# A delta rule's VectorE order, and the last steps of a small inversion on GpSimd, in a float32 transformer kernel

## What is computed

```python
def gated_delta_rule(q, k, v, g, beta):
    ...
    kb = kc * bc[..., None]
    A = jnp.where(strict, jnp.einsum('nbhid,nbhjd->nbhij', kb, kc) * decay, 0.0)
    rhs = jnp.concatenate([vc * bc[..., None], kb * jnp.exp(G)[..., None]], axis=-1)
    sol = lax.linalg.triangular_solve(A + jnp.eye(CHUNK, dtype=A.dtype), rhs, ...)
    ...
    def step(S, xs):
        u_c, w_c, q_c, qk_c, k_c, gl = xs
        v_new = u_c - jnp.einsum('bhck,bhkv->bhcv', w_c, S)
        o = jnp.einsum('bhck,bhkv->bhcv', q_c, S) + jnp.einsum('bhij,bhjv->bhiv', qk_c, v_new)
        S = gl * S + jnp.einsum('bhck,bhcv->bhkv', k_c, v_new)
        return S, o
```

```python
def head_group_norm(t, g):
    mu = jnp.mean(t, axis=-1, keepdims=True)
    var = jnp.mean(jnp.square(t - mu), axis=-1, keepdims=True)
    return (t - mu) * lax.rsqrt(var + NORM_EPS) * g.astype(jnp.float32)
```

## Time and profile before

| | |
|---|---|
| median of 3 runs | 1374.26 us (1373.92 to 1382.46) |
| the profiled execution, its own time | 1378.08 us |
| span of its trace | 1376.3 us |
| busy: PE, PEld, DVE, ACT, POOL | 1286.7, 1097.0, 905.7, 695.6, 103.7 us |
| chain that ended last, by engine | PE 80%, DVE 10%, ACT 5%, POOL 2%, issue 2% |

### The profile page before, as it was taken

How to read it: one execution, slowest core, us unless ns; L and a number is a source line. 1 busy time by engine, 2 the same in 40 slices (tenths; PEclk the granted TensorE clock), 3 DMA queues, 4 the chain that set the end, 5 groups by cost and what they waited for, 6 DMA issues and landing times.

```text
span 1376.3 us, 18712 instructions
## 1 busy us (share of the span) xinstructions
PE 1286.7 (93%) x7504; PEld 1097.0 (80%) x7504; DVE 905.7 (66%) x1395; ACT 695.6 (51%) x1132; POOL 103.7 (8%) x165
## 2 busy tenths in 40 slices
PE   6999999898999999989999999999988879899997
PEld 4899987877888887976888877777877876688886
DVE  4454544346888867676888876755775666666665
ACT  4444444345766655565666755343471114544553
POOL 1000000001000001001000001021370300000000
PEclk9999999999999999999999999999998999999999
DMA  9644333545645557427555547112523105455551
GB/s 352 256 148 165 133 122 129 198 163 215 229 183 184 184 183 269 175 99 292 190 185 184 184 184 265 70 62 105 193 98 92 31 1 182 185 190 185 184 204 65
DMA packets 31780, 231.10 MB, mean 168 GB/s; under 512 B 10912, under 2 KB 14624, under 8 KB 18768
## 3 DMA queue, kind: packets, MB, share of 16 engines
q1 hardware_dynamic: 25616, 218.66, 43.5%
q10 hardware_dynamic: 5072, 7.61, 1.6%
q0 software_dynamic: 1008, 3.67, 0.7%
HBM read 226.22 MB, written 3.71 MB: 167 GB/s over the span
## 4 chain that ended last, share of the span: by engine, by line
PE 80%; DVE 10%; ACT 5%; POOL 2%; issue 2%; DMA 0%; DVEq 0%; POOLq 0%; ACTq 0%
PE ps L425 19%; PE ps L597 15%; PE ps L476 10%; PE ps L197 10%; PE ps L429 10%; PE ps L467 5%; PE ps L564 4%; PE ps L536 3%; PE ps L508 3%; DVE parts L333 2%; ACT parts L329 2%; POOL row L1035 1%; POOL arena L1032 1%; DVE arena L279 1%; ACT arena L231 1%
## 5 line engine op out<-in xcount | busy, mean ns | idle before, releaser
L333 DVE TENSOR_TENSOR parts<-ring,parts 128x1024 fp32r<-128x1024 f32 x354 | 432.9, 1226 | 284.0 <-ACT parts L329 219.2
L329 ACT ACTIVATE parts<-ring 128x1024 fp32r<-128x1024 f32 x354 | 373.2, 1057 | 296.0 <-PE ps L429 107.7
L425 PE MATMUL ps<-hall,parts 128*128 128x512 f32 x1120 | 399.3, 401 | 6.6 <-DVE hall L282 5.1
L429 PE MATMUL ps<-hall,parts 128*128 128x256 f32 x1120 | 315.3, 282 | 0.0
L597 PE MATMUL ps<-parts 128*128 128x512 f32 x1128 | 264.0, 393 | 12.8 <-DVE parts L364 10.6
L597 PEld LDWEIGHTS ps<-parts 128*128 128x128 f32 x1128 | 211.1, 189 | 63.1 <-DVE parts L364 16.4
L425 PEld LDWEIGHTS ps<-hall,parts 128*128 128x128 f32 x1120 | 211.3, 189 | 62.6 <-DVE hall L282 3.5
L429 PEld LDWEIGHTS ps<-hall,parts 128*128 128x128 f32 x1120 | 212.6, 190 | 0.0
L197 PE MATMUL ps<-arena 128*128 128x128 f32 (+3 forms) x1014 | 140.9, 299 | 29.0 <-DVE arena L2037 10.7
L197 PEld LDWEIGHTS ps<-arena 128*128 128x128 f32 (+2 forms) x1014 | 128.0, 194 | 40.0 <-DVE arena L2037 11.3
L476 PE MATMUL ps<-hall,parts 128*128 128x256 f32 x1152 | 140.4, 284 | 0.7 <-ACT arena L1113 0.7
(11 more groups left out here) (229 smaller groups left out, 1066.3 us busy)
## 6 DMA issues: line engine op xcount, KB each, us to landing
ring<-in_W SPq DMA_DIRECT2D x100, 2048.0 KB, 8.1
arena<-distance_tables SPq DMA_DIRECT2D x8, 384.0 KB, 7.9
gains<-in_gains POOLq DMA_DIRECT2D x5, 512.0 KB, 6.5
ring<-in_W SPq DMA_DIRECT2D x4, 512.0 KB, 8.9
arena<-in_gate_w ACTq DMA_DIRECT2D x1, 2048.0 KB, 10.1
matrices<-arena ACTq DMA_DIRECT2D x8, 256.0 KB, 2.8
x<-in_x SPq DMA_DIRECT2D x1, 1024.0 KB, 5.8
gates<-in_ada_gate_b POOLq DMA_DIRECT2D x2, 512.0 KB, 5.3
```

Source lines behind the costliest of these rows:

```text
L329: return nc.scalar.activation(unit_weights(n, 0, weights), weights, ACT.Copy)
L333: return nc.vector.tensor_tensor(unit_weights(n, 1, weights), weights, unit_weights(n, 0, weights), ALU.subtract)
L425: last = nc.tensor.matmul(ps[:, b, :].rearrange("p (a b) -> p a b", a=2), w[:, 0, :], hparts[:, :, k, :], start=k == 0, stop=False)
L429: last = nc.tensor.matmul(ps[:, b, 0:S], w[:, 1, :], hparts[:, 0, k, :], start=False, stop=k == KT - 1)
```

## The change

There are two parts. In the loop the diff reorders VectorE and splits one semaphore:

- the residual R comes behind the level-0 masks and `Rv`, ahead of the level-0 subtractions; so does the retention's centre in step 0
- the level-0 subtraction of `XT` now waits for X·Y alone (PE signals it apart), and each of the two subtractions adds one to `X_out`; PE starts the last level's Y when `XT`'s subtraction is done and does not wait for `X`'s; the last Z (and the query-key products of steps 2 and 3) wait for `X`'s
- nothing stands between the last level's copies and its subtractions. `ET`'s mask follows them; the norm's first half follows them in step 1; the variance and the gates stand at the end of step 0; the norm's other half at the end of step 1; weight splitting late in step 3
- VectorE waits for the step before's `vnew` behind the masks, not ahead of them

In the small inversion GpSimd does all steps: k = 1 to 14, the two `inverse_length`, k = 15 to 30, and the diagonal. ScalarE makes the reversed copy, ahead of the gate's tanh of the retention (`gate_tanh(w_rg, rgt)`), and adds the second `inverses`; SP's first store waits for the first `inverses`, the second store for the second.

```diff
         def first_turned(step, d):
             return 6 * step + 2 * d + 1
         def first_whole(step, d):
             return 6 * step + 2 * d + 2
         def last_turned(step, d):
             return 6 * step + 5 + d
...
-            substitute(1, 11)
+            substitute(1, 15)
             for i in range(TT2, TT2 + TT):
                 inverse_length(i)
-            substitute(11, POOL_STEPS)
+            substitute(15, BLK - 1)
+            nc.gpsimd.memset(WHOLE[:, 0:BLK * BLK:BLK + 1], -1.0).then_inc(S_("inverses"), 1)
...
+            act.wait_ge(S_("inverses"), 1)
+            nc_a.activation(turned_out[SECOND_DIR].rearrange("p i j -> p (i j)"), WHOLE[SECOND_DIR, ::-1], ACT.Copy).then_inc(S_("inverses"), 1)
             act.wait_ge(S_("tok_vector"), TT2 + 2 * TT)
             gate_tanh(w_rg, rgt)
...
-            dve.wait_ge(S_("inverse_step"), 2 * POOL_STEPS - 1)
-            for k in range(POOL_STEPS, BLK - 1):
...
-            link(v.memset(WHOLE[:, 0:BLK * BLK:BLK + 1], -1.0))
-            v.tensor_copy(turned_out[SECOND_DIR].rearrange("p i j -> p (i j)"), WHOLE[SECOND_DIR, ::-1]).then_inc(S_("inverses"), 1)
...
+                for d in DIRS:
+                    xt, xx = half(XT[d], 0, d == 0), half(X[d], 0, d == 1)
+                    dve.wait_ge(S_("Z"), first_turned(step, d))
+                    v.tensor_tensor(xt, xt, half_bank(4 * d + 1, 0, d == 0), ALU.subtract).then_inc(S_("X_out"), 1)
+                    dve.wait_ge(S_("Z"), first_whole(step, d))
+                    v.tensor_tensor(xx, xx, half_bank(4 * d + 2, 0, d == 1), ALU.subtract).then_inc(S_("X_out"), 1)
...
                         if l:
-                            pe.wait_ge(S_("X_out"), level(step, l - 1, d))
+                            pe.wait_ge(S_("X_out"), first_turned(step, d))
...
                         if l == LAST:
+                            pe.wait_ge(S_("X_out"), first_whole(step, d))
...
-                            heads(4 * d + 1, X[d], Ys[l][d])
+                            heads(4 * d + 1, X[d], Ys[l][d]).then_inc(S_("Z"), 1)
                             heads(4 * d + 2, Ys[l][d], X[d]).then_inc(S_("Z"), 1)
...
                 for d in DIRS:
-                    pe.wait_ge(S_("X_out"), level(step, LEVELS - 1, d))
+                    pe.wait_ge(S_("X_out"), last_turned(step, d))
```

98 lines of the change are left out of this document (48 added, 50 removed).

## The result

| | before | after |
|---|---|---|
| median, us | 1380.01 (1373.77 to 1385.78, 7 runs) | 1366.66 (1363.44 to 1369.78, 7 runs) |
| ratio, 95% interval | | 0.9914 (0.9893 to 0.9936) |
| the profiled execution, us | 1378.08 | 1369.78 |

The changed kernel is faster by 0.86%, 11.8 us of 1374, where 18.5 were predicted. The median of the kernel before over these seven runs is 5.75 us above that of the three shown ahead of the prediction, so the ratio is the fairer measure: 1374.26 x 0.9914 = 1362.4 us. The forecast, 1355.8, was too low either way, and the median of 1366.66 lies above the stated range, which ended at 1362.5.

The account below looks back on a forecast made before the run. TensorE idles for VectorE (10.7 us at last-level subtractions, 5.3 at the first `weighed`), then runs at half speed. Inversion 5.9 + loop 10.5 + clock 1.9 and 0.2 = 18.5 us off 1374.26: 1355.8 us, range 1351.3 to 1362.5.

Parts of the forecast that it names:

- Part 1: Small inversion: GpSimd does all steps, so step 0's transposes start earlier; gain 5.9 us, from 3.1 to 7.7.
- the normalizing of the queries: VectorE's reader of the later inverse lengths: delay costs nothing behind a projection, 3 us if that cover fails.
- the clock of step 0: TensorE's half speed in step 0: +1.8 or -1.5 us at about even chances, together +0.2.
- The loop's 1.5 us: Delta loop, step 0: the centre ends earlier, so vnew can start at 1059.3 instead of 1060.78.
- The lower end of my range: Whole kernel: inversion gain at 7.7 us and both clock terms good, 23 us gained, 1351.3 us.
- step 2's miss: Delta loop, step 2: 3.3 us from the wait, less about 0.5 for the later state, 2.8 us gained.
- R ends behind the arrival of Z: Delta loop: sign of being wrong; R was to end at 1073.3 in step 1, hidden behind Z.
- the masks of step 2 wait for VectorE's norm: Delta loop, step 2: sign of being wrong, if a mask waits for the norm.
- Step 1: Delta loop: 4.5 us from the idle time and an earlier Y, plus 1.9 us of clock.
- Step 3: Delta loop: gain of 1.48 + 0.45 = 1.9 us up to vnew.
- The hand-over: Behind step 3's vnew: the weight splitting stands ahead of the output, costing 0.2 us.
- the clock falls in every step all the same: Rival, 12%: small matrices and waits at each level keep half speed; gain 13.4 us, 1360.9 us.

Follow-up runs that it names:

- after_again: The changed kernel itself, measured once more beside its two parts: 1364.2 us, ratio 0.9904.
- whole_wait: The changed kernel, but TensorE's last-level Y waits for both level-0 subtractions of its direction again: 1366.49 us, ratio 0.9917.
- residual_back: The changed kernel with the residual R moved back behind the last copies in steps 1 to 3: 1365.48 us, ratio 0.9909.
- loop_only: The changed kernel with the small inversion of before, so only the delta loop's order is changed: 1366.34 us, ratio 0.9914.
- keys_wait: The changed kernel with GpSimd's decayed keys waiting for both expansions in steps 0 and 2: 1360.49 us, ratio 0.9878.
- centre_early: The changed kernel with the sums and scaling of the retention's centre ahead of step 0's level-0 masks: 1360.87 us, ratio 0.9892.
- combined: The changed kernel with early centre sums, GpSimd's keys waiting in steps 0 to 2, and eight unread multiplications ahead of step 0: 1358.17 us, ratio 0.9863.
- fill_before: The changed kernel with eight unread 128x128 multiplications ahead of the first transposes of step 0: 1362.3 us, ratio 0.9904.
- qk_late: The changed kernel with the query-key products of steps 2 and 3 behind vnew on TensorE's queue: 1365.54 us, ratio 0.9916.
- combined_fill3: As combined, with ten more unread multiplications ahead of the transposes of step 3: 1355.69 us, ratio 0.9832.
- combined_no_fill: As combined, without its unread multiplications: 1362.26 us, ratio 0.9856.

## Why the prediction was wrong

**Part 1** was right as a mechanism and in size. GpSimd's k = 23 to 30 took 1038.13 - 1029.87 = 8.3 us against 8.5, VectorE's first `weighed` starts as scores 0 are done (S + 2.1 us), the four issues take 1.94 us instead of 3.36, and the transposes wait for `expand` and it for the DMAs: 6.1 us between S and T0 against 5.9. That it is so near is partly luck: `expand` starts 0.8 us earlier after S than my sum has it (15.2 against 16.1), since the issues are shorter, and its first half takes longer than the 0.65 us that I had, since the keys are beside it. In `after_again` the gain was 4.8 us. The projection cost 0.7 us (M to S) where I had nothing, and not for the reason that I had weighed: the normalizing of the queries kept its cover, but GpSimd's added steps stand beside VectorE's instructions that read SBUF twice. VectorE's instruction ahead of that projection, before (L1764) and after (L1776), and TensorE behind it:

```profile
997.96 0.69 DVE L1764 TENSOR_TENSOR arena<-arena 128x512 f32<-128x512 f32 x1
```

```profile
1004.33 1.17 DVE L1776 TENSOR_TENSOR arena<-arena 128x512 f32<-128x512 f32 x1
```

```profile
1005.55 11.18 PE L564 MATMUL ps<-parts,hall 128*128 128x512 f32 x48 [1.56 <-DVE arena L1776]
```

TensorE waited 0.67 us there before; the rows do not show more of the cause than that the two engines worked side by side. The other kernels with this inversion have the loss too (46.4 to 46.7 us from M to S, and 48 in `whole_wait` and `residual_back`, against 45.7 and 45.8 for the two without). In the two with 48, TensorE waits 3.14 us at that place and then takes 12.8 us for the same 48 records, not 11.2: clock, where in after none was lost.

**The step that failed is the clock of step 0**: "either can go either way: +1.8 and -1.5 at about even chances, together +0.2". The loop's 1.5 us less the 1.8 us that the step grew makes the term -3.3 us in this trace, and -2.5 in `after_again`. The 3.5 us between +0.2 and -3.3 are half of the 6.9 by which the traces miss the sum. Two things were wrong in it. I took the 1.8 us that half speed cost before as something to be won and 1.5, for which I had no row, as the most that could be lost, though the idle time ahead of the transposes stands ahead of the whole step and not of 32 records; from 14.4 us at full clock the step went up to 19.2, 4.9 us. And I counted the idle time within the step as something that might keep the old loss, not as one that could add to it: the centre ended at 1059.0 and level 0 waited 1.20 us for it, behind which the second stretch fell, 9.26 us against 6.40. `loop_only` has no idle time ahead of the transposes, `keys_wait` less of it (1.29 us), `centre_early` none within the step, and their steps take 14.4, 14.4 and 14.8 us.

More generally, I let gains go through without asking who arrives first where they meet: the inversion's path was still late last, by 2 to 3 us, so all that `weighed` saved beyond it became idle time of TensorE, ahead of a step of small matrices.

The lower end of my range was also added up wrong: 18.5 with 1.8 more of part 1 and 1.6 more of the clock makes 21.9 us, not 23.

**Collisions** in the loop were no term of my sum. `expand` of step 0 (1.3 us in after, none in `after_again`), `expand` ahead of step 2 (2.13 us instead of 1.29, with waits of 0.43 and 0.59 us of TensorE behind it) and L2004 in step 1 (0.54 and 0.99 us instead of 0.15) stand beside GpSimd's keys, whose start moved against VectorE's when the loop became shorter. `keys_wait` gives 0.84 us of step 2 back, `combined` 0.34 of step 1. The rest of step 2's miss (25.2 against the 24.9 predicted) is small.

**Two of my signs of being wrong** came true without costing TensorE a wait that can be seen. R ends behind the arrival of Z in step 1: it ends at 1077.0, 8.4 us behind T1 where I had 7.2, and the first L2020 follows at once, without a wait for Z. And the masks of step 2 wait for VectorE's norm: they start at 1090.21, as the norm's second half ends. TensorE has the keys times the state to do meanwhile, and neither step shows idle time at that place.

**Step 1** saved 5.7 us, against 6.4, with its clock term as predicted: `vnew` follows at once, and the granted clock is 1.00. **Step 3** saved 1.2 in this execution and 3.9 in others, since what I had left out there is a clock term too: it starts behind a wait of 3.09 us for the output, and took 14.65, 16.1 to 16.6 or 17.4 us in the executions seen. The same goes for my scale, the 18.6 us of before, with a clock of 0.91. **The hand-over** cost 0.5 us against 0.2. The rival "the clock falls in every step all the same" comes nearest: its total, 13.4 us, is near the 11.8, but its mechanism, small matrices at each level, is not what the traces show in steps 1 and 2.

**What stays open**: when an idle time of TensorE is followed by half speed and when it is not. In the executions here 1.20 us were followed by half speed in `after`, `after_again` and `fill_before`, and not in `loop_only`, `keys_wait`, `qk_late` and `residual_back`; 1.53 us were in `whole_wait`, with no idle time ahead of the step; 3.09 us ahead of step 3 in some and not in others. The sizes of the losses therefore differ from one execution to the next, and the ratios (nearly all between 0.9904 and 0.9917 for the kernels with this inversion and the late centre) are better evidence than any one of them; they put `keys_wait` and `centre_early` ahead by 2 to 5 us with intervals that overlap, and only `combined_fill3` clearly.

The granted clock of every execution, over its whole span, says a little more. Its mean is 0.978 to 0.980 in the four sets of before, 0.981 and 0.983 in the two of the changed kernel, 0.983 in `loop_only` and 0.986 in `combined_fill3`. If TensorE were busy throughout, 0.001 of it would be 1.4 us of 1370. By that estimate 4 to 7 of the 10 to 11 us between the changed kernel and `combined_fill3` are clock, in all executions together and not in one trace. Between the changed kernel and `loop_only` it tells nothing.

## What to carry to other kernels

When a change removes the wait ahead of one resource, work out who arrives first at the next meeting point and by how much: time that an engine gains and then spends idle ahead of a run of small matrix products can cost, in clock, much of what was saved. Of two independent parts, don't add the gains before asking where one's idle time lands in the other's steps. And when a stage gets shorter, look at what the slow side engine now runs beside: a wait that holds GpSimd back kept `expand` at 1.29 us instead of 2.60, and in that trace the whole step stayed at full clock. And take a loss of clock seen in one trace as one draw: compare several executions before you build on its size.

## What the hardware showed that I had not expected

- A VectorE pair of 1.29 us and a GpSimd pair of 2.04 us, both from SBUF, took 2.60 and 2.48 us side by side; in step 1 two VectorE instructions of 0.15 us took 0.54 and 0.99 beside GpSimd's keys, and those 3.03 instead of 2.04.
- Of the stores and row transfers of `block_inverses` the slowest landed 3.8 to 4.4 us after its issue in most executions, and 4.7, 5.5 and 6.6 us in `combined`, `after_again` and `combined_no_fill`; `expand` started 5.4 us behind the first issue in `keys_wait` and 8.2 in the last.
- What half speed cost behind an idle time did not follow the length of that idle time: 4.71 us of it cost 1.6 us in one execution, 1.82, 0.73 and 1.20 together 4.9 in another. The Trainium skill, "TensorE: Matmul & The Clock Gate", section "HAM oscillation", tells of such a fall for bursts of products that are shorter than the waits between them. Here, and in the steps for which my prediction named it, the waits are shorter than the work around them (1.82 us behind 14.71 in after); the clock fell in step 0 all the same, and in `qk_late` the same code fell less.
